# PEER expert weights on Trainium2: one-hot rows in bf16 with the weight in three parts, in place of 4-byte rows with the weight in two

## The reference, cut to what matters

```python
q = (xb @ w_q).astype(f32).reshape(tb, PEER_HEADS, 2, PEER_DHALF)
s = jnp.einsum('thpd,hpnd->thpn', q, sub_keys.astype(f32))
s_top, i_top = lax.top_k(s, PEER_TOPK)
cand = (s_top[:, :, 0, :, None] + s_top[:, :, 1, None, :])...
best, pos = lax.top_k(cand, PEER_TOPK)
idx = jnp.take_along_axis(cidx, pos, axis=-1)
g = jax.nn.softmax(best, axis=-1)
act = jax.nn.gelu(jnp.einsum('thkd,td->thk', u_tab[idx], xb).astype(f32))
wgt = (g * act).astype(xb.dtype)
return jnp.einsum('thk,thkd->td', wgt, v_tab[idx])
```

## Time and profile before

| | us |
|---|---|
| median of 3 runs | 2134.03 |
| the profiled execution, its own time | 2135.08 |
| its span | 2132.9 |
| PE (matmul) busy | 2067.8 (97%) |
| DVE busy | 1501.6 (70%) |
| ACT busy | 1250.6 (59%) |
| POOL busy | 802.0 (38%) |

### The profile page before, as it was taken

The page is one execution under the profiler, slowest core; times in us unless marked ns, Lnnn a source line. Parts: engine busy times, 40 slices in busy tenths (PEclk is TensorE's granted clock), DMA queues, the critical chain, the costliest instruction groups (busy, mean ns, idle before and its releaser), DMA issues.

```text
span 2132.9 us, 40134 instructions
## 1 busy us (share of the span) xinstructions
PE 2067.8 (97%) x14238; PEld 1834.4 (86%) x14238; DVE 1501.6 (70%) x2698; ACT 1250.6 (59%) x2232; POOL 802.0 (38%) x569
## 2 busy tenths in 40 slices
PE   6999899999999999999998989999999999999998
PEld 3778899999999987777778879999999997777776
DVE  3436579736777778878778563996588887787785
ACT  3534444545666667767754634545566666676774
POOL 1010047754555522223302400688366652222330
PEclk9999999999999999999999989999999999999999
DMA  9745447775555678888864544456544447888883
GB/s 346 278 159 178 151 143 251 239 267 196 188 191 189 201 237 294 296 303 297 296 209 127 153 142 149 147 183 192 189 143 143 138 146 261 299 299 296 297 301 114
DMA packets 125494, 459.95 MB, mean 216 GB/s; under 512 B 14016, under 2 KB 14544, under 8 KB 124352
## 3 DMA queue, kind: packets, MB, share of 16 engines
q1 hardware_dynamic: 102976, 377.14, 52.9%
q0 software_dynamic: 21504, 79.53, 10.1%
q10 hardware_dynamic: 896, 1.76, 0.2%
HBM read 449.93 MB, written 8.44 MB: 215 GB/s over the span
## 4 chain that ended last, share of the span: by engine, by line
PE 92%; DVE 4%; DMA 2%; ACT 1%; issue 1%; SPq 0%; POOL 0%; DVEq 0%; ACTq 0%
PE pu L1332 12%; PE pu L1337 11%; PE pm L1408 11%; PE pm L1410 11%; PE pm L1409 11%; PE pu L1333 11%; PE pu L1202 4%; PE pu L1203 4%; PE pu L1204 4%; PE pm L1367 3%; PE pm L1366 2%; PE pm L1224 1%; PE pm L1672 1%; DMA arena<-in_ada 1%; DVE w_lo L1732 1%
## 5 line engine op out<-in xcount | busy, mean ns | idle before, releaser
L778 ACT ACTIVATE w_hi<-raw 128x1024 fp32r<-128x1024 f32 x600 | 634.0, 1057 | 445.7 <-PE pm L1410 225.4
L1732 DVE TENSOR_TENSOR w_lo<-raw,w_hi 128x1024 fp32r<-128x1024 f32 x444 | 572.3, 1289 | 388.2 <-ACT w_hi L778 377.3
L1332 PE MATMUL pu<-hid_split,w_hi 128*128 128x256 f32 x2048 | 500.3, 285 | 0.0
L1333 PE MATMUL pu<-hid_split,w_hi 128*128 128x256 f32 x2048 | 492.4, 280 | 0.0
L1408 PE MATMUL pm<-w_hi,hid_split 128*128 128x512 f32 x1024 | 405.0, 396 | 3.1 <-DVE hid_split L1995 3.1
L1332 PEld LDWEIGHTS pu<-hid_split,w_hi 128*128 128x128 f32 x2048 | 386.3, 189 | 24.5 <-issue 24.5
L1410 PE MATMUL pm<-w_lo,hid_split 128*128 128x512 f32 x1024 | 403.7, 394 | 0.0
L1409 PE MATMUL pm<-w_hi,hid_split 128*128 128x512 f32 x1024 | 402.9, 394 | 0.0
L1333 PEld LDWEIGHTS pu<-hid_split,w_hi 128*128 128x128 f32 x2048 | 386.1, 189 | 0.0
L577 POOL TENSOR_TENSOR w_lo<-raw,w_hi 128x1024 fp32r<-128x1024 f32 x96 | 229.9, 2396 | 188.4 <-ACT w_hi L778 188.4
L1337 PE MATMUL pu<-hid_split,w_lo 128*128 128x256 f32 x2048 | 290.5, 284 | 0.1
(11 more groups left out here) (276 smaller groups left out, 2931.5 us busy)
## 6 DMA issues: line engine op xcount, KB each, us to landing
raw<-in_u_tab SPq DMA_DIRECT2D x256, 512.0 KB, 3.6
raw<-in_v_tab SPq DMA_DIRECT2D x256, 512.0 KB, 3.5
raw<-in_ada SPq DMA_DIRECT2D x80, 512.0 KB, 3.7
raw<-in_wq SPq DMA_DIRECT2D x32, 512.0 KB, 3.5
raw<-in_gla_in SPq DMA_DIRECT2D x24, 512.0 KB, 4.7
raw<-in_rg_in SPq DMA_DIRECT2D x20, 512.0 KB, 3.5
arena<-in_ada SPq DMA_DIRECT2D x8, 1024.0 KB, 16.7
arena<-in_gla_state POOLq DMA_DIRECT2D x8, 512.0 KB, 14.0
```

What stands on the lines that cost most here:

```text
L778: act.activation(w_hi[:, s2, :], raw[:, s4, :], ACT.Copy).then_inc(hi_done, 1)
L1332: mm(pu[:, s, 0:SEQ], w_hi[:, s % 2, kk * P:kk * P + P], hid_hi[:, kk, 0:SEQ], start=(kk == 0), stop=False)
L1333: mm(pu[:, s, 0:SEQ], w_hi[:, s % 2, kk * P:kk * P + P], hid_lo[:, kk, 0:SEQ], start=False, stop=False)
L1732: tt_(w_lo[:, s2 if l2 is None else l2, :], raw[:, s4, :], w_hi[:, s2, :].bitcast(F32), ALU.subtract).then_inc(lo_done, 1)
```

## The change

The pair matmuls take bf16 operands, and the weight is split into three bf16 parts instead of two 4-byte ones, so each token has 3 matmuls of 128 columns and a chunk has 12.

- Each index, and each of the second and third weight parts, is stored twice side by side as two bf16 numbers in one 4-byte word (`twice`), so that a turned column has the value twice in a row. The one-hot operations read such pairs (`doubled`) with `[4, 64 (step 0), 2]` as their shape, from the banks 0 and 1 of `pm`. The first weight part goes to `sel_w` as before, for ACT.
- `route` has the operations that make the parts, 7 more instructions for each of the two prompt tiles. `turn_slots` turns 5 and 4 arrays in place of 3 and 3, and a last one is turned behind chunk 55 (`turn_last`, `LAST_TURN`).
- DVE multiplies `oh_eq` by the second and third parts (`times_rest`), where POOL multiplied by the rest. POOL instead makes `w_lo` for all late chunks, whole (`late_low`), and DVE for none of them.
- All pair sums go to bank 2, and PE's wait on `w_made` is for the chunk just before. The `ada` steps stay in bank 3.
- ACT applies the gelu of a late chunk ahead of the next `high` instead of behind it.
- `pick_id` and `pick_w` move from `sel_w` to `coef`.

The core of the diff:

```diff
-POOL_ALL = POOL_LOWS + LATE // 2
+POOL_ALL = POOL_LOWS + LATE
+LAST_TURN = 55
-        oh_b = sb("oh_b", [P, TOKS, NKEY], F32R)
-        oh_hi = sb("oh_hi", [P, TOKS, NKEY], F32R)
+        oh_b = sb("oh_b", [P, TOKS, NKEY], BF16)
+        oh_w = sb("oh_w", [P, 3, TOKS, NKEY], BF16)
+        iota_b = sb("iota_b", [P, NKEY], BF16)
...
+        twice = [w.bitcast(BF16).rearrange("p (n d) -> p n d", d=2) for w in part_d]
+        words = [pm[:, 0, 0:SEQ], pm[:, 0, SEQ:2 * SEQ], pm[:, 1, 0:SEQ], pm[:, 1, SEQ:2 * SEQ]]
+        first_p = [pm[:, 1, P:2 * P], pm[:, 1, 3 * P:4 * P]]
+        doubled = [w.bitcast(BF16).rearrange("p (n d) -> p n d", d=2) for w in words]
...
-                def times_low(i, c):
-                    pool.wait_ge(eq_ready, i * 4 + (g0 + c + 1))
...
+                def late_low(i, c, slot):
                     pool.wait_ge(hi_done, i * 4 + (m0 + EARLY + c + 1))
+                    pool.tensor_tensor(w_lo[:, c % 2, :], raw[:, slot, :], w_hi[:, c % 2, :].bitcast(F32),
+                                       ALU.subtract).then_inc(lo_pool, 1)
...
                     times_high(i, c + 1)
                     act.wait_ge(split_used, i * 4 + (m0 + EARLY + c + 1))
+                    gelu_in_place(c)
...
-                    gelu_in_place(c)
...
-                    for a, at in enumerate((pm[:, 1, 0:SEQ], pm[:, 1, SEQ:2 * SEQ], pm[:, 0, 0:SEQ])):
-                        last = pe.transpose(at[:, tt * P:tt * P + P], slot[:, a, :], ident)
-                    last.then_inc(slot_t, 1)
+                    for a in range(4 - tt):
+                        pe.transpose(words[a][:, tt * P:tt * P + P], part_d[a], ident)
+                    pe.transpose(first_p[tt], part_f[:, 0, :], ident).then_inc(slot_t, 1)
...
-                    if not (first and s < 2):
-                        pe.wait_ge(w_made, n - 1)
+                    if not (first and s < 1):
+                        pe.wait_ge(w_made, n)
                     for t in range(TOKS):
-                        out = pm[:, 2 + s % 2, t * P:t * P + P]
-                        mm(out, oh_b[:, t, :], oh_hi[:, t, :], start=True, stop=False)
-                        last = mm(out.rearrange("p (a n) -> p a n", a=4), oh_b[:, t, :], oh_lo[:, t], start=False, stop=True)
+                        out = pm[:, 2, t * P:t * P + P]
+                        for part in range(3):
+                            last = mm(out, oh_b[:, t, :], oh_w[:, part, t, :], start=(part == 0), stop=(part == 2))
...
+                if tt < 2:
+                    for which in range(2):
+                        dve.tensor_copy(twice[which], bc(slot[:, which, :], P, SLOTS, 2))
...
+                    link(dve.tensor_copy(twice[2][:, :, 0], slot[:, 2, :]))
+                    dve.tensor_copy(part_f[:, 0, :], twice[2][:, :, 0])
+                    link(tt_(part_f[:, 1, :], slot[:, 2, :], twice[2][:, :, 0], ALU.subtract))
+                    link(dve.tensor_copy(twice[2], bc(part_f[:, 1, :], P, SLOTS, 2)))
+                    tt_(twice[3], bc(part_f[:, 1, :], P, SLOTS, 2), twice[2], ALU.subtract).then_inc(slot_ready, 1)
...
+                def times_rest(i, c):
+
+                    dve.wait_ge(eq_ready, i * 4 + (g0 + c + 1))
+                    for part in (1, 2):
+                        last = tt_(by_two(oh_w[:, part]), by_two(oh_eq[:]), of_tokens(i, c, part + 1), ALU.mult)
+                    last.then_inc(oh_lo_ready, 1)
...
                     if final < 2:
                         second_hot(i, c + 1)
-                    if c % 2 == 0:
-                        low(i * 4 + (m0 + EARLY + c + 1), slot, 1)
+                        times_rest(i, c + 1)
                     dve.wait_ge(oh_used, i * 4 + (g0 + c + 1))
```

More of the change, by code:

```diff
@@ L620, in late_two @@
[L620 to L624, removed]
-                        low_part(i, c + 2, slot, 1)
-                times_low(0, 0)
-                for part in range(2):
-                    low_part(0, 0, u_load(lay, EARLY)[0], part)
+                    pool.tensor_tensor(w_lo[:, c % 2, :], raw[:, slot, :], w_hi[:, c % 2, :].bitcast(F32),
+                                       ALU.subtract).then_inc(lo_pool, 1)
@@ L630, in peer_pool @@
                 if lay == 0:
-                    for c in range(0, LATE, 2):
-                        late_two(0, c, u_load(0, EARLY + c + 2)[0] if c + 2 < LATE else 0, c + 2 == LATE)
-                else:
-                    with pool.Fori(0, LATE // 4 - 1) as i:
-                        for c in (0, 2):
-                            late_two(i, c, (c + 2) % 4)
-                    late_two(LATE // 4 - 1, 0, 2)
-                    late_two(LATE // 4 - 1, 2, 0, True)
+                    for c in range(LATE):
+                        late_low(0, c, u_load(0, EARLY + c)[0])
+                else:
+                    with pool.Fori(0, LATE // 4) as i:
+                        for c in range(4):
+                            late_low(i, c, c)
@@ L907, in times_high @@
                     for t in range(TOKS):
-                        last = act.activation(oh_hi[:, t, :], oh_eq[:, t, :], ACT.Copy,
-                                              scale=sel_w[:, 0, bass.ds(i * 16 + (c * TOKS + t), 1)].bitcast(F32))
+                        last = act.activation(oh_w[:, 0, t, :], oh_eq[:, t, :], ACT.Copy,
+                                              scale=sel_w[:, bass.ds(i * 16 + (c * TOKS + t), 1)])
                     last.then_inc(oh_hi_ready, 1)
@@ L1942, in peer, with of_tokens, by_two @@
                 dve.wait_ge(slot_t, lay * 2 + 2)
-                link(dve.tensor_copy(sel_w[:, 0, 0:SEQ], pm[:, 0, 0:SEQ]))
-                tt_(sel_w[:, 1, 0:SEQ], pm[:, 0, 0:SEQ], sel_w[:, 0, 0:SEQ].bitcast(F32), ALU.subtract).then_inc(sel_ready, 1)
-                numbers = iota.unsqueeze(1).to_broadcast([P, TOKS, NKEY])
+                dve.tensor_copy(sel_w[:, P:2 * P], first_p[1]).then_inc(sel_ready, 1)
+                numbers = iota_b[:].rearrange("p (x d) -> p x d", d=2).unsqueeze(1).to_broadcast([P, TOKS, NKEY // 2, 2])
+                def of_tokens(i, c, which):
+                    return doubled[which][:, bass.ds(i * 16 + c * TOKS, TOKS), :].unsqueeze(2).to_broadcast(
+                        [P, TOKS, NKEY // 2, 2])
+                def by_two(tile):
+                    return tile.rearrange("p t (x d) -> p t x d", d=2)
                 def first_hot(i, c):
@@ L2026, in peer @@
                     low(m0 + c, u_load(lay, c)[0], c % 2)
+                dve.wait_ge(part_turned, lay + 1)
+                times_rest(0, 0)
                 first_hot(0, 1)
```

81 lines of the change are left out of this document (34 added, 47 removed).

## The result

The changed kernel takes **2115.13 us** (median of 4 runs, 2114.44 to 2116.57) where the kernel before, on the same chip, takes 2134.45 us (2133.92 to 2136.87). The ratio is 0.9907, with a 95% interval of 0.9893 to 0.9921: 19.3 us, or 0.9%, faster. The forecast was 2119 us, in a range of 2108 to 2156.

A forecast was written before the change was run, and what follows sets the result against it. PE was taken to bound the kernel; -15.4 (pair matmuls) + 0.9 (transposes) - 0.3 (way to chunk 48) = -14.8 us against 2135.08 gave 2120.3, and 2119 us for the runs' median, in a range of 2108 to 2156.

The forecast's parts named there:

- What bounds: Late chunks: PE is full, so a chunk costs its PE instructions one behind the other, 3.72 us in layer 1.
- Twelve bf16 pair matmuls: PE, late chunks: twelve at 0.060 us cost 0.72 us against 0.84 for eight 4-byte ones; 15.4 us less in all.
- break-even price of 0.070: PE, late chunks: price in us per bf16 pair matmul at which twelve cost the old 0.84 us.
- The load in line: PE pair matmuls: weight load does not hide behind a short matmul, 0.083 us each; 2155 us in total, chance 14 in 100.
- the full floor: PE pair matmuls: 0.11 us is a floor for any load and matmul with 128 weight columns; 2197 us, chance 10 in 100.
- The wait on w_made: PE before the pair matmuls: 0 us, w_made coming 0.86 us ahead at two elements, 0.08 us at one.
- same sign, less: DVE, layer 1's late chunks: one-element operations and handshakes eat the 0.08 us, 6 us back; 2125 us, chance 7 in 100.
- Two elements at a time with an operand in PSUM: DVE's late-chunk operations: 0.34 us if bf16 pairs run two elements at a time, 0.60 at one; sum holds both ways.
- POOL's w_lo, gelu, ring slots: Late chunks: POOL making every w_lo has 1.7 us of slack with gelu ahead; later slot refills also cost 0.
- Routing: DVE, each prompt tile: 7 more operations, about 2.4 us or some 5 where POOL blocks, hidden under 7.3 us slack: 0.
- DVE's shorter way to chunk 48: DVE, routing to chunk 48 in layer 1: at most 1 us earlier, of which PE takes 0.3 us less.
- Transposes: PE: 10 per layer instead of 6, at 0.11 us each, 0.9 us more in all.

The follow-up runs named there:

- the runs on 64 columns: Only 64 of 128 columns in each pair matmul: the kernel before with its 8 4-byte ones, 2134.69 us; the changed kernel with its 12 bf16 ones, 2078.17 us.
- two banks: The changed kernel with DVE's one-hot operations at one element at a time, plus two banks for the pair sums in layer 1: 2117.82 us.
- the single-element run: The changed kernel with one-hot operations reading only the first of each stored pair, innermost step 0, one element at a time: 2121.49 us.

## Why the prediction was right

- **What bounds.** Right: PE, chunk by chunk. The pitch of layer 1's late chunks fell to 3.55 us, and taking 4 more matmuls out (the run with two parts) shortened the chunks by the price of these matmuls.
- **Twelve bf16 pair matmuls.** The mechanism was right and the size too small: 15.4 us were forecast and 21 came. I took 0.060 us apiece, near what the longer 4-byte matmuls scale to at 0.45 ns per column; the traces show 0.056 within the row of twelve and 0.052 for a matmul left out. The pitch fell by 0.17 us where I had 0.12. The break-even price of 0.070 was further off than the sum had it. The reading of the 0.11 us as a floor of short 4-byte operands is confirmed by the runs on 64 columns. I had drawn it from eight transposes with 64 weight columns; no row then had fewer moving columns, so that part was a guess that came true.
- **The load in line (0.083 us), the full floor (0.111).** Both fell. With 64 columns twelve matmuls took 0.36 us, so no load of that size stands in line. The Trainium skill's page "TensorE: Matmul & The Clock Gate", section "Back-to-back issue gap", has 81 ns for a sustained stream of loads and matmuls of 128 columns; this kernel's stream, with a load in front of each matmul, has 56 ns, and the measurement decides. The same section gives about 56 ns as the gap of a single matmul by itself and says that this is too low for a stream; here the stream met it.
- **The wait on w_made.** Right for the form that ran, where the term is 0. At two elements w_made was to come 0.86 us ahead of need; in the chunk above times_g ends at 1591.11 + 0.68 = 1591.79, 0.89 us ahead of 1592.68. At one element the sum also had 0, with 0.08 us of margin, and that was wrong: it proved too thin and cost 3.0 us, in layer 1 alone. That is the rival "same sign, less" with half its price, and two banks took it back.
- **Two elements at a time with an operand in PSUM.** By the Trainium skill's page "VectorE: DVE Perf Modes", section "The perf-mode tier table", these operations would run at one element per cycle, which the single-element run shows to be 0.68 us. The trace of the change shows 0.42 for 512 elements with an operand in PSUM, and the measurement decides.
- **POOL's w_lo, gelu, ring slots.** 0 as forecast; POOL's 2.39 us are under the pitch, and PE never waits for them in the late chunks.
- **Routing.** This step failed. I put 7 small operations at 2.4 us, 5 where POOL blocks them, under a slack of 7.3. The stretch of the routing that holds them took 10.65 us (from 1374.97 to 1385.62, where L1819 follows) where the same place took 2.0, 8.6 more for one tile. That ate the 7.3 us ahead of the turn and, over two tiles, the 11.8 us ahead of the exponential, and PE waited 1.1 and 1.6 us. The 0.3 us of DVE's shorter way to chunk 48 were lost in it. I had the mechanism in sight, at L1920, but 5 us leave room for about one blocked operation beside the 2.4 us of plain lengths. Three of the new operations waited for almost a whole POOL operation each, and the old L1920 (L1908 now) took 2.14 us instead of 1.56: by the time one was done and the short ones behind it too, POOL's next had begun.
- **Transposes.** 0.9 us were forecast, half of them in the piece between. That piece grew by 2.0 us: 2.4 of new waits net of the 0.3 that stood there, and the rest is within what executions differ by. The transposes were not measured apart, and no run here shows their 0.9 us.

The closeness of the number is in part luck. Against the forecast of 14.8 us the two spans differ by 19.9. The late chunks gave 5.5 us more than forecast (20.9 against 15.4). The piece between gave 1.9 less: it grew by 2.0 us, where the forecast had 0.45 for half of the transposes and -0.3 for chunk 48. The first and the last piece gave 1.5 more: they shrank by 0.4 and 0.6 us, where 0.45 of transposes were forecast, and what made them do so was not tested.

## What to carry to other kernels

Price a matmul by the distance between starts, in its own format and width: here 4-byte ones hardly got cheaper below 256 columns (0.118 us with 256, 0.11 with 128 and with 64) while bf16 ones did with 128 and 64, so three bf16 products beat two 4-byte ones. A vector operation with two SBUF inputs that starts beside a busy POOL can cost what is left of POOL's operation on top of its own length, and so can a cast within SBUF. In a chain of small ones that happens again and again: behind the routing of tile 0 in layer 1 four of the ten waited. For the operation with two inputs, one of them in PSUM freed it. When work is moved into a stretch that only has slack, add up the blocked lengths against every slack behind it, not the first one alone.

## What the runs showed of the hardware that I had not expected

- A 4-byte (fp32r) matmul with 128 weight columns costs 0.11 us with 64 moving columns as with 128; a bf16 one costs 0.030 us with 64 and 0.052 to 0.056 with 128, at a granted clock of 1.00.
- DVE comparing or multiplying 512 bf16 elements with a broadcast operand in PSUM takes 0.42 us when each value is stored twice and read in pairs, and 0.68 when it is read with an innermost step of 0.
- A DVE cast of 128 elements within SBUF (L1911), 0.23 us when it starts in a gap of POOL's, took 2.44 us when it started 0.03 us into a POOL subtraction of 2.39. A DVE subtraction with two SBUF inputs took 0.426 us with POOL out of the way and 2.48 to 2.51 beside it; with one input in PSUM it took 0.424 beside it.
